# Fewer filler matmuls, the Gram matrix in another bank, and a reordered start of the triangular inverse in a hybrid RWKV-7 and mLSTM layer

## The reference, cut to what matters

```python
def step(state, xs):
    r_t, w_t, k_t, v_t, kk_t, b_t = xs
    sa = jnp.einsum('bhvk,bhk->bhv', state, -kk_t)
    state = (state * w_t[:, :, None, :] + sa[..., None] * b_t[:, :, None, :]
             + v_t[..., None] * k_t[:, :, None, :])
    return state, jnp.einsum('bhvk,bhk->bhv', state, r_t)
```

## Time and profile before

| | us |
|---|---|
| median of 3 runs | 3004.61 (3002.61 to 3007.36) |
| profiled execution | 3000.31 |
| its span | 2998.5 |
| TensorE busy in the span | 2891.5 (96%) |
| VectorE, GpSimd, ScalarE busy | 1279.6, 1216.7, 579.6 |
| mean granted TensorE clock | 0.989 of 2.4 GHz |

### The profile page before, as it was taken

The page is one execution under the profiler, slowest core; times in us unless marked ns, Lnnn a source line. Parts: engine busy times, 40 slices in busy tenths (PEclk is TensorE's granted clock), DMA queues, the critical chain, the costliest instruction groups (busy, mean ns, idle before and its releaser), DMA issues.

```text
span 2998.5 us, 38737 instructions
## 1 busy us (share of the span) xinstructions
PE 2891.5 (96%) x15102; PEld 2421.1 (81%) x15102; DVE 1279.6 (43%) x1206; ACT 579.6 (19%) x905; POOL 1216.7 (41%) x651
## 2 busy tenths in 40 slices
PE   7999999999999999969999999999999999999996
PEld 6888888888888888858888887887888888888885
DVE  5431331235556522036676765541454321331334
ACT  3100000002001121125555542110411100000011
POOL 3444333334444366633445443443044433334432
PEclk9999999999999999989999999999999999999998
DMA  3111111113222234331111103321011111111111
GB/s 133 45 46 49 49 49 49 49 44 111 98 98 98 98 111 134 118 90 41 43 33 50 36 15 130 137 70 49 0 49 44 48 49 49 49 49 49 49 40 72
DMA packets 99116, 196.61 MB, mean 66 GB/s; under 512 B 14289, under 2 KB 56401, under 8 KB 98793
## 3 DMA queue, kind: packets, MB, share of 16 engines
q1 hardware_dynamic: 80912, 139.05, 15.4%
q10 hardware_dynamic: 18136, 56.60, 5.0%
HBM read 160.93 MB, written 34.67 MB: 65 GB/s over the span
## 4 chain that ended last, share of the span: by engine, by line
PE 42%; issue 8%; POOL 3%; DVE 2%; ACT 1%; DMA 1%; POOLq 0%; SPq 0%; DVEq 0%; ACTq 0%
PE G L634 12%; PE G L636 12%; PE G L635 12%; PE G L852 2%; PE G L1012 1%; PE G L1035 1%; POOL AL L571 1%; PE G L776 1%; DMA tk<-rows_d 0%; PE G L839 0%; DVE ylo L1838 0%; POOL kap L549 0%; POOL rho L551 0%; DVE xT L1931 0%; POOL ysq L556 0%
## 5 line engine op out<-in xcount | busy, mean ns | idle before, releaser
L592 POOL TENSOR_TENSOR whi<-raw,zero 128x1024 fp32r<-128x1024 f32 (+1 forms) x213 | 398.3, 1870 | 1407.7 <-PE G L636 1404.3
L634 PE MATMUL G<-hhi,whi 128*128 128x512 f32 x2288 | 893.5, 391 | 17.6 <-DVE hlo L1476 17.6
L635 PE MATMUL G<-hlo,whi 128*128 128x512 f32 x2288 | 891.0, 389 | 0.0
L636 PE MATMUL G<-hhi,wlo 128*128 128x512 f32 x2288 | 890.9, 389 | 0.0
L595 POOL TENSOR_TENSOR wlo<-raw,whi 128x1024 fp32r<-128x1024 f32 (+1 forms) x213 | 517.0, 2427 | 16.8
L634 PEld LDWEIGHTS G<-hhi,whi 128*128 128x128 f32 x2288 | 430.0, 188 | 109.0 <-issue 15.2
L636 PEld LDWEIGHTS G<-hhi,wlo 128*128 128x128 f32 x2288 | 430.0, 188 | 89.7
L635 PEld LDWEIGHTS G<-hlo,whi 128*128 128x128 f32 x2288 | 430.1, 188 | 89.4 <-issue 0.7
L634 PE MATMUL G<-ahi,whi 128*128 128x512 f32 x960 | 374.0, 390 | 2.7 <-DVEq L423 2.7
L636 PE MATMUL G<-ahi,wlo 128*128 128x512 f32 x960 | 373.5, 389 | 0.0
L635 PE MATMUL G<-alo,whi 128*128 128x512 f32 x960 | 373.4, 389 | 0.0
(11 more groups left out here) (325 smaller groups left out, 3251.9 us busy)
## 6 DMA issues: line engine op xcount, KB each, us to landing
raw<-in_wg SPq DMA_DIRECT2D x44, 512.0 KB, 3.5
raw<-in_wu SPq DMA_DIRECT2D x44, 512.0 KB, 3.5
raw<-in_wd SPq DMA_DIRECT2D x32, 512.0 KB, 3.5
raw<-in_ml_in SPq DMA_DIRECT2D x16, 512.0 KB, 3.5
zml_d<-po ACTq DMA_DIRECT2D x16, 512.0 KB, 2.6
gates_d<-po ACTq DMA_DIRECT2D x16, 512.0 KB, 2.7
zm<-zml_d SPq DMA_DIRECT2D x8, 1024.0 KB, 5.4
sg<-gates_d ACTq DMA_DIRECT2D x16, 512.0 KB, 5.1
```

Source lines behind the costliest of these rows:

```text
L592: nc.gpsimd.tensor_tensor(hi, raw[:, k, 0:w], zero[:].to_broadcast([P, w]), ALU.add).then_inc(hi_made, 1)
L634: nc.tensor.matmul(dst, wh, hi, start=start, stop=False)
L635: nc.tensor.matmul(dst, wh, lo, start=False, stop=False)
L636: return nc.tensor.matmul(dst, wl, hi, start=False, stop=stop)
```

## The change

- Fillers: the 6 at the top, the 3 ahead of A0, the 2 in each level, the 2 behind yT and the 4 ahead of UQ are taken out; at level 2 three stay instead of four. 31 in an iteration become 3.
- A is written to g0 instead of g1. E of level 1, which writes g0, therefore waits for Aa and Ab; A0 no longer does.
- S goes ahead of var on TensorE.
- VectorE: qe goes from behind Pb to behind bv (and num waits for P now). am0a and am0b come first, am0b waiting for Acb; then U0a, yve, U0b (which waits for Aca), Aa, Pb, Ab, pend.
- ScalarE: the copies Ara and Arb go; in their place it copies both halves of A to Ac (b first, a once am0a is done).
- GpSimd: the masks of level 1 read Ac and not Am; those of levels 1 and 2 go ahead of kw and zg; behind those of levels 3 and 4 it makes Ara and Arb (an addition of zero), ahead of dec.

```diff
-F_ACT = (["P", "Pi", "lnn", "rinv", "atok", "vtok", "btok", "ktok"] + [f"Ar{x}" for x in SETS]
+F_ACT = (["P", "Pi", "lnn", "rinv", "atok", "vtok", "btok", "ktok", "Acb", "Aca"]
...
+    Ac = nc.alloc_sbuf_tensor_at("Ac", [P, NH, SEG], F32, offset=top["mix"] - 3 * NH * SEG * 4)
...
+            def masks(n):
+                for e, x in enumerate(SETS):
+                    part = slice(e * RC, (e + 1) * RC)
+                    if n == 1:
+                        pool.wait_ge(*f_act.at(f"Ac{x}", i))
+                    elif n == 2:
+                        pool.wait_ge(*f_pe.at(f"A0{x}", i))
+                        pool.wait_ge(*f_dve.at(f"A{x}", i))
+                    else:
+                        pool.wait_ge(*f_pe.at(f"W{n - 2}{x}", i))
+                    tt(AL[:, n % 2, part, :], (Ac if n == 1 else Am)[:, part, :], copies(C_LEV + n * P, RC),
+                       ALU.mult).then_inc(*F.sig(f"am{n}{x}"))
+
+            masks(1)
+            masks(2)
             pool.wait_ge(*m_act.at("D", i))
             tt(kw[:], mktok[:], Db[:, :, SEG - 1:SEG].to_broadcast([P, MH, SEG]), ALU.mult).then_inc(*M.sig("kw"))
...
+            for n in range(3, MASKED + 1):
+                masks(n)
+            for e, x in enumerate(SETS):
+                part = slice(e * RC, (e + 1) * RC)
+                tt(Ar[:, part, :], Am[:, part, :], zero[:].unsqueeze(2).to_broadcast([P, RC, SEG]),
+                   ALU.add).then_inc(*F.sig(f"Ar{x}"))
             pool.wait_ge(*m_pe.at("num", i))
...
-                stay_awake(g0[:, 1, :], 6)
...
-                gram(alpha, beta, g1).then_inc(*F.sig("A"))
+                gram(alpha, beta, g0).then_inc(*F.sig("A"))
+                pe.wait_ge(*m_act.at("ktok", i))
+                for h in range(MH):
+                    last = nc.tensor.matmul(m0[:, h * SEG:(h + 1) * SEG], zm[:, MH + h, :], zm[:, h, :], start=True,
+                                            stop=True)
+                last.then_inc(*M.sig("S"))
...
-            stay_awake(g2[:, 0, :], 3)
             for e, x in enumerate(SETS):
                 pe.wait_ge(*f_dve.at(f"am0{x}", i))
-                pe.wait_ge(*f_dve.at(f"A{x}", i))
...
-                    pe.wait_ge(*m_dve.at("qe", i))
+                    pe.wait_ge(*m_dve.at("P", i))
...
-                    stay_awake(g0[:, 1, :], 2)
...
-                    stay_awake(g0[:, 1, :], 4)
+                    stay_awake(g0[:, 1, :], 3)
...
-                stay_awake(g0[:, 1, :], 2)
                 pe.wait_ge(*f_act.at(f"Tc{n}a", i))
+                if n == 1:
+                    pe.wait_ge(*f_dve.at("Aa", i))
...
-            stay_awake(g0[:, 0, :], 4)
...
-            for e, x in enumerate(SETS):
-                act.wait_ge(*f_dve.at(f"A{x}", i))
-                activation(half(Ar, e), half(Am, e), ACT.Copy).then_inc(*F.sig(f"Ar{x}"))
+            act.wait_ge(*f_pe.at("A", i))
+            activation(half(Ac, 1), g0[:, 1, :], ACT.Copy).then_inc(*F.sig("Acb"))
+            act.wait_ge(*f_dve.at("am0a", i))
+            activation(half(Ac, 0), g0[:, 0, :], ACT.Copy).then_inc(*F.sig("Aca"))
...
+                if e:
+                    dve.wait_ge(*f_act.at("Acb", i))
+                tt(AL[:, 0, four(e), :], three(g0[:, e, :]), copies(C_LEV, RC), ALU.mult).then_inc(*F.sig(f"am0{x}"))
+            first(0)
             if back:
                 output_variance()
-            first(0)
+            dve.wait_ge(*f_act.at("Aca", i))
             first(1)
+            lower(0)
             dve.wait_ge(*m_act.at("D", i))
             dve.wait_ge(*m_pe.at("S", i))
             stt(flat(Pb[:]), m0, ML_SCALE, flat(Db[:]), ALU.mult, ALU.mult).then_inc(*M.sig("P"))
...
+            lower(1)
+            tt(pend[:], Pp[:, :, DEC - 1:DEC], con(C_ONES, 1).unsqueeze(1).to_broadcast([P, RC, 1]),
+               ALU.mult).then_inc(*F.sig("pend"))
```

More of the change, by code:

```diff
@@ L106 @@
         + ["F", "V", "B", "UQ", "Wst", "Z", "gate"])
-F_ACT = (["P", "Pi", "lnn", "rinv", "atok", "vtok", "btok", "ktok"] + [f"Ar{x}" for x in SETS]
+F_ACT = (["P", "Pi", "lnn", "rinv", "atok", "vtok", "btok", "ktok", "Acb", "Aca"]
          + [f"{y}{n}{x}" for n in range(1, LEVELS) for x in SETS for y in ("Wc", "Tc")] + ["Tc", "W1c", "Zc", "gev"])
 F_DVE = (["dec", "scan", "hend", "cc", "gs", "av", "gu", "kmod", "ssc", "n1", "n2", "rin", "kk", "kka",
-          "alpha", "beta", "bv", "pend"] + [y for x in SETS for y in (f"am0{x}", f"A{x}")] + ["U0a", "U0b"]
+          "alpha", "beta", "bv", "am0a", "am0b", "U0a", "U0b", "Aa", "Ab", "pend"]
          + [y for n in range(1, LEVELS) for y in [f"U{n}a", f"U{n}b"] + LATE.get(n, [])] + ["Q", "S0s", "B", "Uf"])
-F_POOL = ["rk", "rkb", "kap", "rho"] + [f"am{n}{x}" for n in range(1, MASKED + 1) for x in SETS]
+F_POOL = ["rk", "rkb", "kap", "rho"] + [f"am{n}{x}" for n in range(1, MASKED + 1) for x in SETS] + [f"Ar{x}" for x in SETS]
 B_PE = ["U", "Y", "dS", "mean", "var"]
@@ L118 @@
 M_ACT = ["E", "nm", "ktok", "vtok", "D", "aden", "lnv", "rsv"]
[L119 removed]
+M_DVE = ["qe", "P", "dmax", "rec", "hm", "st", "mv", "ve", "C", "g1", "g2", "g3", "yn", "y1"]
 M_POOL = ["arg", "kw", "zg", "dec"]
@@ L563, in iteration @@
             tt(zm[:, 12:16, :], zm[:, 12:16, :], vbc("ml_norm", SEG), ALU.mult).then_inc(*M.sig("zg"))
-            for n in range(1, MASKED + 1):
-                for e, x in enumerate(SETS):
-                    if n == 1:
-                        pool.wait_ge(*f_dve.at(f"A{x}", i))
-                    else:
-                        pool.wait_ge(*f_pe.at(f"A0{x}" if n == 2 else f"W{n - 2}{x}", i))
-                    part = slice(e * RC, (e + 1) * RC)
-                    tt(AL[:, n % 2, part, :], Am[:, part, :], copies(C_LEV + n * P, RC),
-                       ALU.mult).then_inc(*F.sig(f"am{n}{x}"))
+            for n in range(3, MASKED + 1):
[4 more added lines that the diff above has]
+                   ALU.add).then_inc(*F.sig(f"Ar{x}"))
             pool.wait_ge(*m_pe.at("num", i))
@@ L841, in iteration @@
                 return
-            pe.wait_ge(*m_act.at("ktok", i))
-            for h in range(MH):
-                last = nc.tensor.matmul(m0[:, h * SEG:(h + 1) * SEG], zm[:, MH + h, :], zm[:, h, :], start=True, stop=True)
-            last.then_inc(*M.sig("S"))
             def four(dst, e, left, right):
@@ L906, in iteration @@
                 pe.wait_ge(*f_act.at(f"Tc{n}b", i))
+                if n == 1:
+                    pe.wait_ge(*f_dve.at("Ab", i))
                 four(g0, 1, Tr, lambda n: Wr[:, n, :]).then_inc(*F.sig(f"E{n}b"))
@@ L1707, in iteration @@
                 tt(bv[:], three(g0[:, 1, :]), zs[:, 8:12, :], ALU.mult).then_inc(*F.sig("bv"))
+                dve.wait_ge(zm_in, i * 16 + 16)
+                dve.wait_ge(*m_act.at("E", i))
+                stt(flat(qe[:]), zm[:, 0:MH, :].rearrange("p h t -> p (h t)"), ML_SCALE, flat(Eb[:]), ALU.mult,
+                    ALU.mult).then_inc(*M.sig("qe"))
             if back:
@@ L1715, in iteration @@
             dve.wait_ge(*f_pe.at("A", i))
-            tt(pend[:], Pp[:, :, DEC - 1:DEC], con(C_ONES, 1).unsqueeze(1).to_broadcast([P, RC, 1]),
-               ALU.mult).then_inc(*F.sig("pend"))
             def four(e):
@@ L1738, in update, with lower @@
                 block.then_inc(*done)
+            def lower(e):
+                nc.vector.copy_predicated(Am[:, four(e), :], copies(C_LOW, RC).bitcast(U32),
+                                          three(g0[:, e, :])).then_inc(*F.sig(f"A{SETS[e]}"))
             for e, x in enumerate(SETS):
-                tt(AL[:, 0, four(e), :], three(g1[:, e, :]), copies(C_LEV, RC), ALU.mult).then_inc(*F.sig(f"am0{x}"))
-                nc.vector.copy_predicated(Am[:, four(e), :], copies(C_LOW, RC).bitcast(U32),
-                                          three(g1[:, e, :])).then_inc(*F.sig(f"A{x}"))
+                if e:
+                    dve.wait_ge(*f_act.at("Acb", i))
+                tt(AL[:, 0, four(e), :], three(g0[:, e, :]), copies(C_LEV, RC), ALU.mult).then_inc(*F.sig(f"am0{x}"))
+            first(0)
             if back:
                 output_variance()
-            first(0)
+            dve.wait_ge(*f_act.at("Aca", i))
             first(1)
+            lower(0)
             dve.wait_ge(*m_act.at("D", i))
```

5 lines of the change are left out of this document (1 added, 4 removed).

## The result

| | before | after |
|---|---|---|
| median (lowest to highest), us | 3004.25 (3002.61 to 3007.36), 4 runs | 3059.0 (3044.26 to 3086.59), 4 runs |
| ratio, 95% interval | | 1.0195 (1.0153 to 1.0237) |
| profiled execution, its span | 3000.31, 2998.5 | 3044.57, 3042.8 |
| mean granted clock | 0.989 | 0.965 |

What follows compares the result with a forecast made beforehand. TensorE was taken as busy 433.76 of over 460 us in the loop, partly with unread fillers, its successors often awaiting other engines. -2.1 us a segment, -17 in eight, plus 7 for the clock gave 2995 us, range 2983 to 3009.

Steps and rivals of the forecast that it cites:

- Part 7: The clock in the loop: falls to 1.2 GHz cost 0.9 us a segment, +7 us, between 0 and 18.
- rival 3: Slower by the clock alone: two dear falls a segment, at alpha turn and value matmuls, 3015 us; chance 0.10.
- one dear and one cheap: Clock falls: dear on A, mean, turns or value matmuls, 1.5 to 1.8 us; cheap in level 5, 0.3 to 0.5.
- Rival 1: The clock holds in the loop: 2988 us, down to 2980 if the queues bind less; chance 0.27.
- Rival 2: Falls eat the gain: one dear and one cheap a segment, 2.2 us against 2.1, 3005 us; chance 0.20.
- Rival 4: Change hardly acts: dec so late that level 5 begins as now, -0.5 us a segment, 3001 us; chance 0.08.
- Part 1: Six fillers at the top: 0 us; the wait ahead of the alpha turn grows from 0.47 to about 1.7.
- Part 2: Gram matrix A to level 1: -1.05 us, level 1's two fillers included; qe's move hidden.
- Part 3: Levels 2 and 3: -0.75 and about +0.1 us, with small VectorE instructions waiting up to one GpSimd mask.
- Part 4: GpSimd's queue: dec late, at 1535.6 to 1536.1, with C and level 5 behind it; W5a 1.55 us earlier.
- Parts 5 and 6: Levels 5 and 6: 0 and -0.5 us; the four fillers ahead of UQ: 0.

Runs made afterwards that it cites:

- e4: Kernel after with the fillers outside the levels back (6 at the top, 3 ahead of A0, 4 ahead of UQ); 3071.75 us, ratio 1.0206 to before.
- e1: Kernel before with 28 of its 31 fillers a segment out (3 left in level 2), nothing moved; 3007.94 us, ratio 1.0012 to before.
- e12: Kernel after with its own three fillers, both Ar copies back on ScalarE and dmax reading PSUM; 3064.3 us, ratio 1.0216 to before.
- e5: Kernel before with all fillers in segment 0 and three a turn later; 2995.23 us, ratio 0.9974 to before.
- e6: e5 plus, in later turns, fillers beside other work (6 top, 2 each in levels 4 and 5, 3 ahead of UQ); 2992.55 us, ratio 0.9965 to before.
- e10: e9 with two more fillers in level 3 and two ahead of yT; 2984.92 us, ratio 0.9947 to before.
- e11: e6 with a fourth filler in level 2, two in level 3 and one ahead of yT; 2999.72 us, ratio 0.9984 to before.
- e8: Kernel after with the fillers of e6, one behind A0, one in level 1, and both Ar copies back on ScalarE; 2999.56 us, ratio 0.998 to before.
- e9: e8 with dmax reading PSUM, as two VectorE instructions in place of ScalarE's absolute value and one; 2982.5 us, ratio 0.993 to before.

## Why the prediction failed, by its steps

**The step that failed is Part 7, the clock**: its direction was right, its size was not. It took 0.9 us a turn, with 2.2 as the upper end. In the profiled execution it was 10.9 and 2.35 us in turns, and 12.8 in segment 0 (70.95 against 58.2), 7.5 us a turn over the seven. Three things in it were wrong.

1. *The price in the levels.* Part 7 put a low stretch in level 5 at 0.3 to 0.5 us, since by the earlier trace rows VectorE ends last there. But the four matmuls of a level take 0.45 us at one clock and 0.86 at the other, and a level has six such groups in line; once they slow down, TensorE ends last, and the norm's queue on VectorE covers nothing. From dC to UQ the low clock costs 9.9 us in 23.9. Part 7 priced A by its length at the other clock; it never asked what happens to a whole level when each of its matmuls doubles. (Of its two figures for A at 2.4 GHz, 1.16 is A's; the 1.09 is from the turn of px in the attention.)
2. *The length.* Every case in the list, rival 3 included, was made of falls that pass: one dear and one cheap, or two dear. None had a clock that stays low over 24 us while TensorE works. The earlier trace rows showed a fall between turns with nothing around it, and was read as the pattern for the loop. The trace of before had another pattern, in segment 0, where the clock is low for 6.8 us and TensorE busy for 6.1 of them; its second half by windows:

```profile
1336.00:1340.00 4.00, 4.00 (x26) 3.68 (x25) 2.35 (x5) 2.23 (x6) 2.32 (x3) 0.50 0.00 0
```

3. *The place.* The alpha turn was named as the place most like the earlier trace rows. Falls do occur there, 3.4 us long and 1.06 us dear. e4 has none of them and is as slow as after. The place that mattered is the stretch of 128-column matmuls from level 4 to behind F. Part 7 had named it too, the wait ahead of yT, and took it for the cheap one. That wait was put at about 1.5 us and is 0.25 at most; the 1.1 us of the long turns stands ahead of W4a.

**Rival 3** (slower, by the clock alone) had the sign and the cause, and a chance of 0.10; its time was 3015 against 3059.0, since it had two falls of 1.7 us a turn. Its sign, A or the value matmuls at twice their length, came half: A keeps its 1.16 us in every turn, but the value matmuls take 3.40 us instead of 1.75 in segments 2, 4 and 6, close to the price that rival 3 gave them. Those turns are 60.6 us all the same, level with before. The loss of the kernel stands in the turns with the long stretch in the levels, which rival 3 did not have. **Rival 1** (the clock holds, 2988) is what the same walk would give: with the clock at 1.00, e1's and after's steps make 58.1 and 58.2 us a turn. **Rival 2** (falls eat the gain, 3005) describes the short turns alone. **Rival 4** fell: dec was not late.

The Trainium skill, page "TensorE: Matmul & The Clock Gate", section "Why this matters for your kernels", which Part 7 weighed, is contradicted further: after idles for at most 1.70 us at once in the loop and runs at 0.86. Another section of the same page of the Trainium skill, "A second HAM failure mode: psum-queue depth-cycling", tells of short, frequent idle times between groups of matmuls that let the clock swing between its levels; that agrees with the alternating turns of after, and was overlooked in the prediction. It tells nothing of what such a swing costs in a loop like this one, where the table above has it.

**Part 1** holds: the wait ahead of the alpha turn was put at about 1.7 and is 1.70; at full clock the step to A keeps its length.

**Part 2** holds at its front: A to W1a was put at -1.3 (its own times give -1.4) and came at -1.53, and qe's move is hidden (VectorE still waits 1.45 us for the mean). It was put down to the new order as a whole, though: e1 gets -0.24 of it without moving anything, and of the rest the new order keeps only 0.69 by num, since E1a now waits 0.2 to 0.6 us for ScalarE's copies of level 1, which stand behind its two root operations (W1a to num +0.60). For A to num the parts gave -1.05 and the trace gives -0.89 (8.68 to 7.79).

**Part 3** had levels 2 and 3 at -0.65 together, num to dC. Measured -0.38. The fillers there are worth -1.10 (e1) and dmax takes back 0.72. Part 3 had the mechanism, a small VectorE instruction that waits up to one mask, and took 0.1 us for it where it is 0.7. The earlier trace rows had shown pend at 0.73 for four elements: that was the size to take. So W3a came at -1.3, where -1.8 was forecast, and W4a at -0.5, where -1.7 was (both in the short turn, less the 2.36 us of its low piece ahead of them).

**Part 4** was wrong. Its walk had masks at 1.30, Ar copies at 1.05 to 1.30, and dec as the last of the queue at 1535.6 or later. dec is done 2.6 us ahead of C in after (1494.84 and 1497.44), as the masks came at 1.25 and the copies at 1.02. C stands on VectorE behind the norm statistics and the updates of level 3, and these behind dmax: that is the late one. The -1.55 at W5a came nevertheless near, at -1.4, since yT and level 5 hang on that queue and not on W4a. (A to Mu is -1.83; Mu also loses the two fillers of level 5 ahead of it, which the norm on VectorE covers.)

**Parts 5 and 6** hold nearly: level 5 keeps its length (W5a to W6a 4.81 us before, 4.82 after), and level 6 loses 0.42 (W6a to F 5.12 and 4.70) where 0.5 was forecast. Mu to F hides this in the table (+0.03), as Mu itself moved against both. F is at -1.80, forecast -2.05, and F to Wst gives -0.23 where 0.05 was expected. The sum, -2.1 a turn, is right at -2.0, partly by errors that cancel.

**What stays open.** Why the clock falls in one turn and not in the next of the same order isn't settled. e1 and e12 have the same three fillers; e1 runs most turns at 1.00, e12 with shorter turns goes low in segment 2 and in each turn from there. Idle time ahead of dC is ruled out as the whole cause by e12, and the idle time ahead of the alpha turn by e4. No run has both short waits everywhere and few fillers, so idle time in sum isn't ruled out. That the cycle locks in by turns is seen in after and e12, and not explained. Why segment 0 goes low for longer than the others without its fillers (41 us in e1, 10 with them in e5) was not followed up. The PSUM reading of dmax was not tried in the old order, where dmax takes 0.44 us without the fillers (e1).

## What to carry to other kernels

A filler matmul is priced by two things: what its successor would have waited for anyway (beside other work it is free, as in e6, and in line it costs 0.23 us, as in e10 and e11), and what the loop would cost at the lower clock, which is read by doubling each matmul of the stretch and asking who ends last then. Before fillers are taken out for their time, run the kernel once without them and read the clock of the first segment and of the loop; the answer holds for that order alone, as e1 and e12 show. Here keeping the free ones and dropping the ones in line gave 0.35%, and dropping nearly all in a new order lost 2%. When work moves onto GpSimd, list the small VectorE instructions with two SBUF operands that will run beside it, and give one of their operands in PSUM if it comes from there.

## What the runs showed of the hardware

The clock stays at 1.2 GHz for 23.9 us while TensorE is busy for 23.39 of them (window at 1557.20 of after), and for 30.7 while it is busy for 30.20 (window at 1491.25 of e4): being busy with 128-column matmuls did not bring it back there. A microsecond at that level costs the loop 0.31 us at the alpha turn (1.06 for 3.4), 0.35 at the value matmuls and level 2 (2.35 for 6.8), 0.41 from dC to UQ (9.9 for 23.9) and 0.40 over a turn of e12 (11.0 for 27.3).

Executions of one program differ by 42 us (after, 3044.26 at 0.964 and 3086.59 at 0.947), where 24 of before stay within about 11 us. By these clocks the longer one was low for some 108 us more, an estimate from the means, and 42 us for 108 is 0.39 a microsecond, the price above. A median of few runs of such a kernel tells less than its clocks.

A VectorE instruction of four elements a partition that reads two SBUF operands takes 0.16 us with GpSimd idle or between two of its instructions, and up to 1.34 while it works (dmax in before and e8); with one operand in PSUM it always takes 0.16 (e9). The Trainium skill, page "SBUF — State Buffer", section "SBUF: two separate sides", says that VectorE and GpSimd share a port pair under an exclusive lock, and that a VectorE instruction with two SBUF inputs and a GpSimd instruction that reads SBUF block each other for a whole instruction. The trace agrees: the 1.34 us in e8 end 0.02 us behind the end of a whole mask of 1.27, and the dmax of e1, which meets dec on its way, ends 0.02 us behind dec.
